# Reordering the first pair of a seven-product up projection, the last pair's additions, and the queue of the megabyte weight loads

## The reference, cut to what matters

```python
def sq_relu_mlp(xn, w_up, w_down):
    return jnp.square(jax.nn.relu(xn @ w_up)) @ w_down
```

## Time and profile before

| | |
|---|---|
| median of 3 runs | 1552.16 us (1551.59 to 1554.86) |
| the profiled execution | 1554.59 us, span of the core 1552.8 us |
| busy in the span | TensorE 1525.7 us (98%), VectorE 952.2 (61%), ScalarE 590.1 (38%), GpSimd 250.6 (16%) |
| mean granted TensorE clock | 0.995 |
| up projection in pairs | from 875.5 us of the span to 1205.3 us |
| down projection | from 1205.3 us to the end |

### The profile page before, as it was taken

The page is one execution under the profiler, slowest core; times in us unless marked ns, Lnnn a source line. Parts: engine busy times, 40 slices in busy tenths (PEclk is TensorE's granted clock), DMA queues, the critical chain, the costliest instruction groups (busy, mean ns, idle before and its releaser), DMA issues.

```text
span 1552.8 us, 26644 instructions
## 1 busy us (share of the span) xinstructions
PE 1525.7 (98%) x10896; PEld 1451.3 (93%) x10896; DVE 952.2 (61%) x1345; ACT 590.1 (38%) x1015; POOL 250.6 (16%) x329
## 2 busy tenths in 40 slices
PE   9999999999999999999999899999998999999999
PEld 8999999986768999986899899999998999999999
DVE  7646777757677443446343966666665578646653
ACT  7421031236675221235222633333433433333332
POOL 1010000002000100000000054455543311010110
PEclk9999999999999999999999999999999999999999
DMA  8435111103101533021222154433344865354563
GB/s 276 139 107 174 42 42 41 45 1 121 47 28 68 160 134 128 14 83 59 84 85 80 49 180 156 155 145 142 132 157 179 286 229 192 108 188 123 174 215 106
DMA packets 63038, 189.32 MB, mean 122 GB/s; under 512 B 7888, under 2 KB 12040, under 8 KB 62784
## 3 DMA queue, kind: packets, MB, share of 16 engines
q1 hardware_dynamic: 37280, 91.11, 18.4%
q0 software_dynamic: 25648, 96.65, 17.2%
HBM read 138.58 MB, written 54.12 MB: 124 GB/s over the span
## 4 chain that ended last, share of the span: by engine, by line
PE 49%; DMA 3%; DVE 2%; issue 1%; POOL 1%; ACT 1%; DVEq 0%; ACTq 0%; POOLq 0%
PE ps L2723 20%; PE ps L2744 18%; PE ps L417 6%; DMA a<-wdn 2%; PE ps L2607 2%; PE ps L2579 2%; DVE t_raw L2004 1%; DMA w_raw<-wdn 1%; DMA quads_d<-quad_sum 0%; PE ps L2589 0%; DVE t_lo L2009 0%; POOL Y L961 0%; DVE wq_lo L2034 0%; DVE stat_row L503 0%; DVE hid_stage L1981 0%
## 5 line engine op out<-in xcount | busy, mean ns | idle before, releaser
L417 PE MATMUL ps<-A_hi,w_hi 128*128 128x364 f32 x768 | 172.4, 333 | 0.3 <-DVE Y L1507 0.3
L417 PE MATMUL ps<-A_hi,w_lo 128*128 128x364 f32 x768 | 169.4, 329 | 0.0
L417 PE MATMUL ps<-A_lo,w_hi 128*128 128x364 f32 x768 | 169.2, 328 | 0.0
L381 ACT ACTIVATE w_hi<-w_raw 128x1024 fp32r<-128x1024 f32 x42 | 44.2, 1058 | 288.7 <-PE ps L417 187.3
L417 PEld LDWEIGHTS ps<-A_hi,w_hi 128*128 128x128 f32 x768 | 131.6, 188 | 7.3 <-issue 6.5
L417 PEld LDWEIGHTS ps<-A_lo,w_hi 128*128 128x128 f32 x768 | 133.6, 188 | 0.0
L417 PEld LDWEIGHTS ps<-A_hi,w_lo 128*128 128x128 f32 x768 | 133.4, 188 | 0.0
L385 DVE TENSOR_TENSOR w_lo<-w_raw,w_hi 128x1024 fp32r<-128x1024 f32 x42 | 51.1, 1221 | 103.2 <-ACT w_hi L381 103.2
L2723 PE MATMUL ps<-t_hi,wq_hi 128*128 128x272 f32 x480 | 101.6, 293 | 8.1 <-issue 4.1
L2723 PE MATMUL ps<-t_lo,wq_hi 128*128 128x272 f32 x480 | 101.1, 292 | 0.0
L2723 PE MATMUL ps<-t_hi,wq_lo 128*128 128x272 f32 x480 | 100.7, 291 | 0.0
(11 more groups left out here) (313 smaller groups left out, 3552.0 us busy)
## 6 DMA issues: line engine op xcount, KB each, us to landing
w_raw<-slabs SPq DMA_DIRECT2D x67, 512.0 KB, 3.8
quads_d<-quad_sum POOLq DMA_DIRECT2D x64, 272.0 KB, 2.9
w_raw<-wdn POOLq DMA_DIRECT2D x32, 512.0 KB, 4.0
r_raw_a<-quads_d SPq DMA_DIRECT2D x56, 272.0 KB, 3.0
r_raw_b<-quads_d SPq DMA_DIRECT2D x56, 272.0 KB, 2.9
quads_d<-hid_stage POOLq DMA_DIRECT2D x48, 272.0 KB, 3.0
Y<-xT POOLq DMA_DIRECT2D x16, 546.0 KB, 4.6
y_d<-Y POOLq DMA_DIRECT2D x16, 546.0 KB, 3.2
```

The costliest lines, as they stand in the source:

```text
L381: e.activation(WH[:, par], RAW[:, par], ACT.Copy).then_inc(s.w_hi, 1)
L417: ins = e.matmul(PS[:, 3 * par + c, 0:CH], wt[:, wpar, w], xt[:, col:col + CH], start=(first and n == 0 and m == 0), stop=(last and n == l ...
```

## The change

Three edits. First, the first pair's products run in the order 0, 3, 1, 2, 5, 4, then product 0 of the second pair (number 7), then 6; the slots and the semaphore counts follow the position (`POS`), and the lists of ScalarE and VectorE for these products are written out. The first three quarter sums of the two plain tiles (`hp = 0`) are taken by VectorE (`quad_sums_std`) instead of GpSimd, which no longer waits for `t_lo` before it starts `quads(0)`; the loads of the second pair's weights wait for `t_f` instead of `t_lo`. Second, at the seam VectorE does `combine` and `relu` of products 101 and 102 and `combine(103)` ahead of `down_lo(0)`, and SyncE issues `a11_load(0)` ahead of `right_load(4)` to `right_load(7)`. Third, the four `ZA21` loads move from GpSimd to SyncE, behind `right_load(9)`, `(11)`, `(13)` and `(15)`, and GpSimd's `stream_load(0)` and `(1)` move ahead of the four loads of `Y`.

```diff
+TURN = [0, 3, 1, 2, 5, 4, 7, 6] + list(range(8, N_PROD))
+POS = {q: n for n, q in enumerate(TURN)}
...
                 elif p == 1:
-                    sp.wait_ge(s.t_lo, 16)
+                    sp.wait_ge(s.t_f, 16)
                     sp.wait_ge(s.y2_out, 16 * KT)
                 else:
-                    sp.wait_ge(s.sp_lo, 7 * (p - 1))
+                    sp.wait_ge(s.sp_lo, 7 * (p - 1) + (1 if p == 2 else 0))
...
+            def a21_load(z):
+                sp.wait_ge(s.prod, N_PROD)
+                if z:
+                    sp.wait_ge(s.a21_in, 16 * z)
+                sp.dma_start(ZA21[z][:, :, 0:512], wdn[W_A21 * KD + 4 * z:W_A21 * KD + 4 * z + 4]
+                             .rearrange("k p c -> p k c")).then_inc(s.a21_in, 16)
...
-            sp.wait_ge(s.prod, N_PROD - 5)
-            for n in range(4, 8):
-                right_load(n)
             sp.wait_ge(s.prod, N_PROD - 4)
             a11_load(0)
+            for n in range(4, 8):
+                right_load(n)
...
                 right_load(n)
+                if n in (9, 11, 13, 15):
+                    a21_load((n - 9) // 2)
...
-            g.wait_ge(s.t_lo, 16)
             for hp in range(KD):
                 quads(hp)
+            g.wait_ge(s.sp_lo, N_PROD)
+            stream_load(g, 0)
+            stream_load(g, 1)
...
-            g.wait_ge(s.sp_lo, N_PROD)
-            stream_load(g, 0)
-            stream_load(g, 1)
-            g.wait_ge(s.prod, N_PROD)
-            for z in range(4):
...
             act_bcast(e, cnt, RSTD)
+            left_hi(3)
+            t_hi(2)
+            hidden_std(0)
             left_hi(1)
-            hidden_std(0)
+            prod_copy(0)
+            left_hi(2)
             hidden_std(1)
-            left_hi(2)
-            t_hi(2)
...
+            t_hi(3)
+            left_hi(5)
+            left_hi(4)
+            prod_copy(1)
+            left_hi(7)
+            prod_copy(2)
+            left_hi(6)
...
+            def quad_sums_std():
+
+                b11, b12, b22 = HST[:, 0, 0:HT], HST[:, 0, HT:2 * HT], HST[:, 1, HT:2 * HT]
+                e.wait_ge(s.u_sq, 2)
+                e.tensor_tensor(TQ[0][:, :], b12, b11, ALU.subtract).then_inc(s.q_t, 1)
+                e.wait_ge(s.q_t, 1)
+                e.tensor_tensor(TQ[1][:, :], b22, TQ[0][:, :], ALU.subtract).then_inc(s.q_t, 1)
+                e.tensor_tensor(TQ[2][:, :], b22, b12, ALU.subtract).then_inc(s.q_t, 1)
...
-            left_sum(1)
             e.wait_ge(s.bc_used, cnt.used(cnt.bc))
             relu_std(0)
+            left_lo(3)
+            relu_std(1)
+            left_sum(1)
+            left_sum(2)
             left_lo(1)
-            relu_std(1)
-            left_sum(2)
             t_lo(1)
...
+            left_lo(2)
+            left_sum(5)
+            left_sum(4)
+            left_lo(5)
+            left_lo(4)
+            t_lo(2)
+            left_lo(7)
+            quad_sums_std()
+            t_lo(3)
+            left_lo(6)
+            combine(3)
+            combine(4)
+            left_sum(8)
+            left_lo(8)
+            combine(5)
...
+            combine(N_PROD - 4)
+            relu(N_PROD - 4)
+            combine(N_PROD - 3)
+            relu(N_PROD - 3)
+            combine(N_PROD - 2)
+            down_lo(0)
+            relu(N_PROD - 2)
+            combine(N_PROD - 1)
+            for n in range(1, 4):
+                down_lo(n)
...
+                    if p == 0:
+                        e.wait_ge(s.tile_read, S_UP + 2)
...
-            for q in range(N_PROD):
+            for q in TURN:
                 product(q)
```

More of the change, by code:

```diff
@@ L937, in quads @@
                     g.wait_ge(s.t_out12, 32 * hp)
-                g.tensor_tensor(TQ[0][:, :], b12, b11, ALU.subtract).then_inc(s.q_t, 1)
+                    g.tensor_tensor(TQ[0][:, :], b12, b11, ALU.subtract).then_inc(s.q_t, 1)
                 g.wait_ge(s.q_t, 4 * hp + 1)
-                g.tensor_tensor(TQ[1][:, :], b22, TQ[0][:, :], ALU.subtract).then_inc(s.q_t, 1)
-                g.tensor_tensor(TQ[2][:, :], b22, b12, ALU.subtract).then_inc(s.q_t, 1)
+                if hp:
+                    g.tensor_tensor(TQ[1][:, :], b22, TQ[0][:, :], ALU.subtract).then_inc(s.q_t, 1)
+                    g.tensor_tensor(TQ[2][:, :], b22, b12, ALU.subtract).then_inc(s.q_t, 1)
                 g.dma_start(rd[R_T1, hp], TQ[0][:, :]).then_inc(s.t_out0, 16)
@@ L1351, in prod_copy @@
                     return
-                e.wait_ge(s.prod, q + 1)
+                e.wait_ge(s.prod, POS[q] + 1)
                 if p:
@@ L1359, in left_hi @@
                 p, i = divmod(q, 7)
-                if q < 2:
+                n = POS[q]
+                if n < 2:
                     e.wait_ge(s.tile_done, S_UP + 1)
-                elif q < 4:
+                elif n < 4:
                     e.wait_ge(s.tile_done, S_UP + 2)
                 else:
-                    e.wait_ge(s.prod, q - 3)
+                    e.wait_ge(s.prod, n - 3)
                 if i in (0, 3):
@@ L1370, in left_hi @@
                 else:
-                    e.wait_ge(s.sp_sum, 4 * p + {1: 1, 2: 2, 4: 3, 5: 4}[i])
-                e.activation(WQ[0][:, q % 4], left(p, i), ACT.Copy).then_inc(s.sp_hi, 1)
+                    e.wait_ge(s.sp_sum, 4 * p + ({1: 1, 2: 2, 5: 3, 4: 4} if p == 0 else {1: 1, 2: 2, 4: 3, 5: 4})[i])
+                e.activation(WQ[0][:, n % 4], left(p, i), ACT.Copy).then_inc(s.sp_hi, 1)
             def hid_square(q):
@@ L1405, in _ @@
             act_bcast(e, cnt, RSTD)
+            left_hi(3)
+            t_hi(2)
+            hidden_std(0)
             left_hi(1)
-            hidden_std(0)
+            prod_copy(0)
+            left_hi(2)
             hidden_std(1)
-            left_hi(2)
-            t_hi(2)
[L1411 to L1419, removed]
-                    down_hi(q - N_PROD)
-                if q >= 5:
-                    hid_square(q - 5)
+            t_hi(3)
[5 more added lines that the diff above has]
+            left_hi(6)
+            for q in (8, 9):
+                left_hi(q)
+            for q in range(10, N_PROD + 5):
+                if q < N_PROD + 4:
+                    prod_copy(TURN[q - 4])
+                if q < N_PROD:
+                    left_hi(q)
+                else:
+                    down_hi(q - N_PROD)
+                if q == 10:
+                    for i in (3, 4, 5):
+                        hid_square(i)
+                if q >= 12:
+                    hid_square(TURN[q - 5])
             for n in range(5, N_STEP):
@@ L2032, in left_lo @@
                 p, i = divmod(q, 7)
-                e.wait_ge(s.sp_hi, q + 1)
-                e.tensor_tensor(WQ[1][:, q % 4], left(p, i), WQ[0][:, q % 4].bitcast(F32), ALU.subtract)\
+                n = POS[q]
+                e.wait_ge(s.sp_hi, n + 1)
+                e.tensor_tensor(WQ[1][:, n % 4], left(p, i), WQ[0][:, n % 4].bitcast(F32), ALU.subtract)\
                     .then_inc(s.sp_lo, 1)
@@ L2115, in _ @@
             t_raw(2)
-            left_sum(1)
             e.wait_ge(s.bc_used, cnt.used(cnt.bc))
             relu_std(0)
+            left_lo(3)
+            relu_std(1)
+            left_sum(1)
+            left_sum(2)
             left_lo(1)
-            relu_std(1)
-            left_sum(2)
             t_lo(1)
[L2123 to L2126, removed]
-                    left_sum(q + 1)
[L2128 to L2135, removed]
+            left_lo(2)
[13 more added lines that the diff above has]
+            combine(5)
+            left_sum(9)
+            relu(3)
+            left_lo(9)
+            relu(4)
+            relu(5)
+            for q in range(10, N_PROD):
+                combine(TURN[q - 4])
+                if q + 1 < N_PROD:
+                    left_sum(q + 1)
+                left_lo(q)
+                relu(TURN[q - 4])
+            combine(N_PROD - 4)
[8 more added lines that the diff above has]
+                down_lo(n)
             for n in range(4, N_STEP):
@@ L2691, in product @@
                 p, i = divmod(q, 7)
-                e.wait_ge(s.sp_lo, q + 1)
+                n = POS[q]
+                e.wait_ge(s.sp_lo, n + 1)
                 if i == 0:
@@ L2708, in product @@
                 elif i == 3:
-                    if p:
+                    if p == 0:
+                        e.wait_ge(s.tile_read, S_UP + 2)
+                    else:
                         e.wait_ge(s.u_add, 3 * p - 2)
@@ L2722, in product @@
                         for c in range(2):
-                            ins = e.matmul(PS[:, b + c, 0:HC], WQ[wx][:, q % 4, k * P:(k + 1) * P], right(i, xx, k, c),
+                            ins = e.matmul(PS[:, b + c, 0:HC], WQ[wx][:, n % 4, k * P:(k + 1) * P], right(i, xx, k, c),
                                            start=(i in (0, 1, 3) and k == 0 and m == 0),
```

## The result

Changed kernel: median 1541.48 us (1539.66 to 1542.75, 6 runs). Kernel before, beside it: 1554.03 us (1551.59 to 1554.97, 6 runs). The ratio is 0.9915, interval 0.990 to 0.993: 12.6 us between the medians, where 17.8 was forecast, and 1541.5 is above the range's end of 1540.0. Of the 7.1 us between 1541.5 and the forecast 1534.4, 5.2 are gain that is missing and 1.9 the kernel before, whose median was 1552.16 over three runs when the forecast was made and is 1554.03 here.

The account below looks back on a forecast made before the run. TensorE is busy nearly throughout, so only its three MLP stalls can give time: 6.5 + 6.6 + 4.7 = 17.8 us, taking the median from 1552.16 to 1534.4 us. Range 1532.8 to 1540.0.

Parts of the forecast that it names:

- What a stall costs: TensorE's MLP stalls: each costs more than its idle time because slow clock follows, so priced start to start against 3.02 us products.
- the three stalls of before: Start of the up pairs 6.78 us, seam 6.60, down step 19 4.69; together 18.1 us, the ceiling of the gain.
- Part 1: First pair of up products: reordering removes the 6.78 us stall except 0.3 us ahead of product 6, gaining 6.5 us.
- the grid: TensorE's unstalled schedule: product starts 3.02 us apart from 875.54, if nothing is late.
- Part 2: Seam from up to down projection: down(0) starts on time even at the old load landing, gaining 6.6 us, bounds 4.0 and 6.6.
- Part 3, the stream load: Down step 19: stream_load(2) released some 39 us behind down(0) instead of 49, removing the stall and gaining 4.7 us.
- step 19's stall: Down projection: TensorE loses 4.69 us because VectorE's sum for step 20 waits for stream_load(2); assumed wholly recoverable.
- Part 3, the moved loads: ZA21 loads on SyncE: first issued at 7.6 us behind down(0), landing near 20; right_load(12) keeps 4 us, no stall.
- The fourth: Rival, down projection: zone loads on SyncE hold back right operands, losing 24 us against 17.8 gained, time 1558; chance 2%.

Follow-up runs that it names:

- experiment 3: Changed kernel with the four ZA21 loads issued behind right_load(13), (15), (17), (19); ratio to the kernel before 0.9903, down projection 339.0 us.
- 11: Changed kernel with the ZA21 loads behind right_load(11), (13), (15), (17); ratio to the kernel before 0.9894, down projection 339.0 us.
- 12: Changed kernel with the ZA21 loads issued by ScalarE in a queue of their own; ratio to the kernel before 0.9902, down projection 339.0 us.
- experiment 5: Kernel of experiment 3 with GpSimd's fourth quarter sum of the plain tiles waiting for combine(4); ratio to the kernel before 0.9895.
- 6: Kernel of experiment 3 with SyncE's old seam order, right_load(4) to (7) ahead of a11_load(0); ratio to the kernel before 0.9898.
- experiment 7: Kernel of experiment 3 with VectorE's old seam order, down_lo(0) ahead of combine(102); median 1543.35 us, ratio to the kernel before 0.9931.
- experiment 2: Changed kernel with the ZA21 loads back on GpSimd ahead of the third stream load; ratio to the kernel before 0.9947, down projection 346.6 us.
- experiment 1: Kernel before with only the first-pair edits, seam order and both load lists as before; ratio to the kernel before 0.9969.
- experiment 4: Changed kernel with each of GpSimd's first four Y loads split into two transfers of half the columns; ratio to the kernel before 0.9925.
- experiment 10: Changed kernel, unchanged, traced and timed again; ratio to the kernel before 0.9917, down projection 343.1 us.

## Why the prediction was wrong, point by point

- **What a stall costs.** Right in the traces: priced from start to start, the three stalls of before were 18.1 us, and 17.6 was found in the traces of experiments 3, 11 and 12. The medians of those runs gained 14.4 to 16.3.
- **Part 1.** Right. Product 6 was 0.42 us late from start to start, 0.3 forecast; the cause named (GpSimd's fourth quarter sum) was confirmed by experiment 5. Product 3 was within 0.15 us of the grid.
- **Part 2.** Right in size and mechanism, by experiments 6 and 7. But the first `ZA11` load took 8.45 us in its new place, not 5.3 to 6. That cost nothing here and was paid in part 3.
- **Part 3, the stream load.** Right in mechanism: step 19's stall is gone, `stream_load(2)` is issued 47.5 us behind down(0) in the changed kernel. I had said 39: the released sum stood behind low parts that waited for right operands. In experiment 3 it was 39.4.
- **Part 3, the moved loads.** This is the step that failed: "the first `ZA21` load is issued at 7.6 ... and lands near 20; ... 4 us are left. No stall." It was issued 11.9 us behind down(0) and landed at 28.5. The cost was put at nothing and was 4.7 us: 343.7 against 339.0. Two terms were wrong. The issue was 4.3 us late, mostly because the `ZA11` loads, each issued when the one before had landed, took 8.45, 7.50 and 5.64 us, where I had taken 5.3 to 6. The landing took 16.7 us, not 12.4: the fourth `ZA11` load (10.4 us) and two right operands were still in the queue ahead. The even share that I had assumed was about right over those 16.7 us (3.15 of 6.06 MB), but they ran at 364 GB/s, not 399, and GpSimd's queue took 65% once its `Y` loads were there, more than the "up to half" of the forecast. Then I tested `right_load(12)`, which stands behind the second zone load, and not `right_load(10)` and `(11)`, which stand behind the first, the one that meets the stores of the last quarters, two stream loads and four `Y` loads.
- **The rivals.** The fourth was the mechanism: the zone loads hold the right operands back. I priced it only at its worst, 24 us with a chance of 2%, and gave its mild form, one landing of 16.7 us instead of four of 13, neither a price nor a chance. So the range ended at 1540.0, with 1541.5 measured.
- **The step-19 stall in the sum.** 4.7 us was its price in one trace. It was 7.6 with the seam mended (experiment 2) and none in one execution with part 1 alone (experiment 1). The parts do not add.

## What to carry to other kernels

A large load that is needed late does not belong in the queue of small loads that are needed soon, even when the count of bytes fits: put it behind the small ones that fall due while it runs, or in another queue. Either way the load itself still took 16.0 and 14.6 us. Look also at what the issuing engine waits for between its issues: a wait for one large load to land holds back the issue of every small one behind it. Test the first small transfer behind the first large one, at the time when the other queue is fullest, not the average. When a transfer's landing is near the limit, its price from one trace is not its price in the median.

## What the runs showed of the hardware

- How two busy queues shared the DMA engines changed within one load. SyncE's queue (2048- and 2176-byte rows) moved 2.05 of 2.90 MB before GpSimd's `Y` loads (4368-byte rows) were issued, and 1.10 of 3.16 MB with them there, at 406 GB/s. Why is not shown: halving the rows (experiment 4) decided nothing.
- TensorE's clock did not fall behind every idle stretch of about 2 us. Idle 1.80 us was followed by granted 0.62 and 0.53 in the changed kernel; 1.61 us in experiment 7 and 1.98 us in experiment 4 by 1.00, the 2.4 GHz level throughout; and 2.07 us in experiment 10, at the same step as in experiment 4, by 0.71 over the 4 us shown here, with 0.50, the 1.2 GHz level, from 1247 to 1249:

```profile
1247.00:1251.00 4.00, 4.00 (x25) 4.00 (x24) 3.93 (x7) 1.32 (x3) 0.73 (x1) 0.71 0.41 128
```

- A GpSimd sum of two SBUF operands held up VectorE's subtractions of two SBUF operands: four `t_lo` took 3.79 us with one of 1.58 us beside them and 2.62 without, 1.2 us more.
